# Moving the small tables and the bfloat16 constants ahead of the weight ring in SBUF

## The reference, cut to what matters

```
def sqrelu_mlp(h, w_up, w_down):          # 1024 -> 4096 -> 1024, twice
    u = jax.nn.relu(h @ w_up)
    return (u * u) @ w_down
proj = h @ w_in                           # dsa_mixer
r, k, v = jnp.einsum('cbld,cde->cble', xs[:3], w_rkv)   # rwkv7_mixer
split(h @ w_in, ...)                      # conv: 4 x 1024 columns, dilated: 8 x 1024 columns
```

## The kernel before

| tensor | start | past a whole KB |
|---|---|---|
| `raw`, `w_hi`, `w_lo` (16 KB each) | 16,512, 32,896, 49,280 | 128 |
| `X`, `const`, `const_bf` (3,328 B) | 65,664, 73,856, 86,144 | 128 |
| `gate`, `scale_row`, `pcol` | 89,472, 97,664, 101,760 | 384 |
| `mod_col` to `less_k_a` (small) | 102,688 to 103,072 | mixed |
| `per_head` | 103,104 | 704 |
| `act_f`, `act_hi0`, `act_lo0`, `act_hi1`, `act_lo1` (8 KB each), `xn` over them | from 104,128 | 704 |
| `ff_hi`, `ff_lo`, `qk` and others of the stages | from 145,088 | mostly 704 |

## Time and profile before

### The profile page before, as it was taken

One profiled execution on the slowest core, in us unless ns is written; L12 is line 12 of the kernel. 1 busy time (PEld: TensorE's weight loads), 2 busy tenths in 40 slices (PEclk: granted clock), 3 DMA queues, 4 the chain that ended last, 5 costly groups with the idle time before them and its releaser, 6 DMA issues.

```text
span 1066.7 us, 25458 instructions
## 1 busy us (share of the span) xinstructions
PE 1048.1 (98%) x10480; PEld 996.2 (93%) x10485; DVE 771.7 (72%) x1090; ACT 590.3 (55%) x900; POOL 120.4 (11%) x131
## 2 busy tenths in 40 slices
PE   9999999999999999999999999999999999999997
PEld 8966999999999899997899999999998999999985
DVE  5987666766789689768766676786676877775586
ACT  6586555555456783334555454564544667666452
POOL 0230010100000028841000000000000000000000
PEclk9999999999999999999999999999999999999999
DMA  8734687888634510002678777737653656556401
GB/s 308 251 90 137 216 286 266 271 296 280 204 122 155 163 61 5 3 11 74 217 250 287 255 252 264 276 121 228 197 192 112 212 181 199 171 195 196 143 2 59
DMA packets 83073, 192.23 MB, mean 180 GB/s; under 512 B 6000, under 2 KB 6912, under 8 KB 82992
## 3 DMA queue, kind: packets, MB, share of 16 engines
q1 hardware_dynamic: 74256, 159.93, 45.3%
q0 software_dynamic: 7584, 27.53, 7.8%
q10 hardware_dynamic: 1152, 3.59, 1.0%
HBM read 189.45 MB, written 1.05 MB: 179 GB/s over the span
## 4 chain that ended last, share of the span: by engine, by line
PE 88%; DVE 6%; issue 2%; ACT 2%; DMA 2%; POOL 0%; DVEq 0%; POOLq 0%; ACTq 0%
PE bank L2308 13%; PE bank L2310 13%; PE bank L2309 13%; PE bank L2659 5%; PE bank L2658 5%; PE bank L2660 5%; PE bank L2325 4%; PE bank L2345 4%; PE bank L2877 4%; PE bank L2275 2%; PE bank L2276 2%; PE bank L2277 2%; PE bank L2263 1%; PE bank L2265 1%; PE bank L2264 1%
## 5 line engine op out<-in xcount | busy, mean ns | idle before, releaser
L1350 DVE TENSOR_TENSOR w_lo<-raw,w_hi 128x1024 fp32r<-128x1024 f32 x295 | 357.8, 1223 | 199.2 <-ACT w_hi L737 198.7
L737 ACT ACTIVATE w_hi<-raw 128x1024 fp32r<-128x1024 f32 x295 | 310.3, 1059 | 291.4 <-PE bank L2310 150.4
L2308 PE MATMUL bank<-act_hi,w_hi 128*128 128x256 f32 x1200 | 334.0, 278 | 0.4 <-DVE w_lo L1350 0.3
L2309 PE MATMUL bank<-act_lo,w_hi 128*128 128x256 f32 x1200 | 332.9, 277 | 0.0
L2310 PE MATMUL bank<-act_hi,w_lo 128*128 128x256 f32 x1200 | 332.8, 277 | 0.0
L2308 PEld LDWEIGHTS bank<-act_hi,w_hi 128*128 128x128 f32 x1200 | 225.3, 188 | 1.7 <-DVE w_lo L1350 0.9
L2310 PEld LDWEIGHTS bank<-act_hi,w_lo 128*128 128x128 f32 x1200 | 225.3, 188 | 0.0
L2309 PEld LDWEIGHTS bank<-act_lo,w_hi 128*128 128x128 f32 x1200 | 225.0, 187 | 0.0
L2658 PE MATMUL bank<-w_hi,ff_hi 128*128 128x256 f32 x512 | 141.5, 276 | 0.0
L2659 PE MATMUL bank<-w_lo,ff_hi 128*128 128x256 f32 x512 | 141.5, 276 | 0.0
L2660 PE MATMUL bank<-w_hi,ff_lo 128*128 128x256 f32 x512 | 141.5, 276 | 0.0
(11 more groups left out here) (375 smaller groups left out, 1675.4 us busy)
## 6 DMA issues: line engine op xcount, KB each, us to landing
raw<-in_mlp_w_up_dram SPq DMA_DIRECT2D x64, 512.0 KB, 3.7
raw<-in_mlp_w_down_dram SPq DMA_DIRECT2D x64, 512.0 KB, 6.1
raw<-in_dil_w_in_dram SPq DMA_DIRECT2D x64, 512.0 KB, 4.1
mod_w<-in_w_mod_dram POOLq DMA_DIRECT2D x48, 512.0 KB, 5.9
raw<-in_conv_w_in_dram SPq DMA_DIRECT2D x32, 512.0 KB, 4.5
raw<-in_rwkv_w_rkv_dram SPq DMA_DIRECT2D x24, 512.0 KB, 4.1
raw<-in_dsa_w_in_dram SPq DMA_DIRECT2D x12, 512.0 KB, 8.1
raw<-in_dsa_w_o_dram SPq DMA_DIRECT2D x8, 512.0 KB, 4.5
```

The lines of the kernel that those rows point to most:

```text
L737: act.activation(w_hi[:, slot, :], raw[:, slot, :], ACT.Copy).then_inc(hi_ready, 1)
L1350: dve.tensor_tensor(w_lo[:, slot, :], raw[:, slot, :], w_hi[:, slot, :].bitcast(F32), ALU.subtract).then_inc(lo_ready, 1)
L2308: pe.matmul(dst, w_hi[:, slot, at], hi[:, kt, :], start=begin, stop=False, skip_group_check=True)
L2309: pe.matmul(dst, w_hi[:, slot, at], lo[:, kt, :], start=False, stop=False, skip_group_check=True)
```

## The change

The allocations of `pcol`, `mod_col`, `gain`, `c_col`, `stat`, `half_neg`, `less_k_a` and `const_bf` are moved ahead of `raw`. Nothing else is touched: no instruction, no order, no wait, no shape.

```
+        pcol = sb("pcol", [P, PARAM_COLS])
+        mod_col = sb("mod_col", [P, 2, 2 * KT])
+        ... gain, c_col, stat, half_neg, less_k_a
+        const_bf = sb("const_bf", [P, n_const_bf], BF16)
         raw = sb("raw", [P, RING, GRAN])
         ... scan_a, glora laid over w_hi and w_lo
         w_hi = sb("w_hi", [P, RING, GRAN], F32R)
         w_lo = sb("w_lo", [P, RING, GRAN], F32R)
         X = sb("X", [P, TILES, D])
         const = sb("const", [P, n_const])
-        const_bf = sb("const_bf", [P, n_const_bf], BF16)
         gate = sb("gate", [P, 2, D])
         scale_row = sb("scale_row", [P, D])
-        pcol = sb("pcol", [P, PARAM_COLS])
-        ... mod_col, gain, c_col, stat, half_neg, less_k_a
         per_head = sb("per_head", [P, SEQ])
```

More of the change, by code:

```diff
@@ L165, in program @@
         bank = [keep.enter_context(nc.psum_tensor(f"bank{b}", [P, BLOCK], F32)) for b in range(8)]
+        pcol = sb("pcol", [P, PARAM_COLS])
+        mod_col = sb("mod_col", [P, 2, 2 * KT])
+        gain = sb("gain", [P, 2, KT])
+        c_col = sb("c_col", [P, KT])
+        stat = sb("stat", [P, 26])
+        half_neg = sb("half_neg", [P, 2])
+        less_k_a = sb("less_k_a", [P, KT])
+        n_const_bf = sum(int(np.prod(v.shape[1:])) for v in parts_bf.values()) - TILES * SEQ
+        const_bf = sb("const_bf", [P, n_const_bf], BF16)
         raw = sb("raw", [P, RING, GRAN])
@@ L190, in program @@
         n_const = sum(int(np.prod(v.shape[1:])) for v in parts.values())
-        n_const_bf = sum(int(np.prod(v.shape[1:])) for v in parts_bf.values()) - TILES * SEQ
         const = sb("const", [P, n_const])
-        const_bf = sb("const_bf", [P, n_const_bf], BF16)
         gate = sb("gate", [P, 2, D])
         scale_row = sb("scale_row", [P, D])
[L196 to L202, removed]
         per_head = sb("per_head", [P, SEQ])
```

## The result

| kernel | median us | runs, us | against the kernel before, 95% interval |
|---|---|---|---|
| before | 1062.27 | 1061.30 to 1068.49 (4) | 1 |
| after | 1094.66 | 1094.29 to 1095.77 (4) | 1.0295 [1.0267, 1.0324] |

The change makes the kernel 3% slower. The forecast was no net change, 1063 us, with a range up to 1077. The measured time lies 18 us above its upper end, on the side that was given the smaller chance (0.24 for slower, 0.29 for faster).

What follows compares the result with a forecast made beforehand. The prediction took TensorE's cadence of successive products as the bound. No net change gave 1066.7 + 0 = 1066.7 us of span, carried over as a difference to 1063 us, with a range of 1048 to 1077 us.

Steps and rivals of the forecast that it cites:

- splitting, VectorE, plain float32 and the queues: Work outside split products: no cost from new addresses; at most 0.07 us on VectorE's L1426, which is not the bound.
- The two cadences at equal addresses: Split products of 256 columns: 117.7 ns in the dilated attention, 113.0 in the convolution, with the same code, tensors and addresses.
- the direct effect on the cadence: Some 6,400 split products on TensorE: moving weights to distance zero from the activations was taken to cost 0 us.
- The nearest row: The indexer's products, weights 288 B apart between slices: 117 ns, taken as the nearest evidence for distance zero.
- The bounds: All split products at the short cadence, 11.2 us less, or all at the long one, 16.3 us more.
- Modulo 512: Feature-form split products: distance alternates between 576 and 64 B with one cadence, so it could count only modulo 512 B.
- All short: Split products: alignment removes the long cadence, 11.2 us less, 1052 us; chance 0.17.
- the excess vanishes: Split products run at a plain float32 pass's pace, 46 us less, 1017 us; chance 0.12 for this or a good part.
- The MLPs stay long: Both MLPs keep the long cadence without flips, 11.2 us more, 1074 us; chance 0.16, another 0.08 for up to 1079.
- The odd pair at distance zero: MLP change from feature to token form: activations stream while ff_hi loads; this pair's address match might explain the cadence flip.
- The reshuffled cadences: Stages swap long and short cadence by less than 10.6 us, or no net change: chance 0.47, forecast 1063 us.
- The rule: TensorE reads streaming operand and next weights through independent ports, so distance cannot matter: no change; not relied on.

Runs made afterwards that it cites:

- map_forms: Separate kernel of only float32r products in an MLP step's order, at eight weight-to-activation distances: 120.0 ns at distance 0, 113.5 or 117.9 ns at 192 B.
- tables_ahead: Against the kernel before, only the small tables (1,344 B) moved ahead of the ring, const_bf left in place: 1095.34 us, ratio 1.0301.
- mod_col_ahead: Against the kernel before, only mod_col (128 B) moved ahead of the ring: 1071.93 us, ratio 1.0062.
- map_distance: Separate kernel of only float32r products, stepping the bytes by which the stationary operand lies past the streaming one: 120.0 ns at 0, 117.8 at 64 and mostly at 192.

## Why the prediction was wrong

**Right: what bounds the kernel.** It was read from the cadence of products and not from waits or busy shares, and the whole result lies in that cadence. That splitting, VectorE, plain float32 and the queues cost nothing is confirmed term by term: 1223 and 1059 ns became 1224 and 1057, L1426 and L2841 did not move. The two cadences at equal addresses are real and come back without the rest of the kernel (`map_forms`).

**The step that failed** is the one on the split products: "I therefore take **0 us** for the direct effect on the cadence." It measured +6.66 ns for each of 3,665 products and +2.21 for 2,367, and -6 for each wide one: 24.4 + 5.2 - 2.0 = +27.6 us. Four things in it were unsound.

- *The row's operands do not move.* The indexer's weights and the activations both lie behind `per_head` and keep their addresses. Its cadence is 117 ns before and after and says nothing on a change of distance.
- *The nearest row was not near.* Its products pass through distances in steps of 32 B and load 72 columns. The map shows that fewer loaded columns can take away the penalty at zero (120.0 with 128 columns, 113.4 with 64), and a mean over many distances hides the value at one. So 117 ns could not stand for distance zero.
- *The bounds were not bounds.* "The bounds are the two pure cases" took the two cadences seen today as the ends, -11.2 and +16.3 us. A row shows what holds at its own addresses. For a distance with "no steady stretch" in the trace nothing excluded a third value. The text named it as what would make the forecast wrong ("a third value") and gave it neither price nor chance.
- *Modulo 512 was the coarsest reading.* Within a granule the distance alternates between 576 and 64 B with one cadence; that allows 512 or any divisor of it. It is 256. This did not hurt the forecast of this change, as zero is zero by either, but it would have mispriced `tables_ahead`.

**The rivals.** *All short* and *the excess vanishes* had the sign wrong for the 256 columns; in the wide products alone 6 of the 16 ns did go. The observation against the latter, that wide products pay most although the load is beside only a part of them, was sound. Its price rests on 108 ns as the pace of a pass, which is half of the measured 217 and was not itself measured; the trace records each plain float32 product of the program as two (16 calls, 32 records in the earlier trace rows). No series came to it. *The MLPs stay long* had the sign right and half of the mechanism: at distance zero nothing flips any more and one cadence goes through both MLPs, 181 us each. It put that cadence at 117.8 ns; it is 120.0, in all stages. Even its farthest end, 1079, was 16 us short. The odd pair at distance zero that was to explain the flip does not by itself make one: where the token form gives way to the feature form, streaming weights meet loading weights, also at distance zero modulo 256, and the kernel before has no flip there. The reshuffled cadences that carried the chance of 0.47 exist, at the distance 64 of `mod_col_ahead`, and are worth +0.6% there.

**The rule.** By the Trainium skill (TensorE: Matmul & The Clock Gate, Part 2: What happens when you issue a matmul) streaming operand and next weights are read through two independent ports, and the load takes nothing from the stream. The maps contradict for float32r what follows from it: the same instructions take 120.0 or 113.3 ns, by their distance modulo 256 B. Whether the ports themselves or something behind them is shared, no run shows. I had seen that the trace did not agree (two cadences at equal addresses) and yet drew the rule's conclusion.

**Shown and argued.** Shown: the distance sets the cadence, with period 256 B; 0 gives 120.0 ns; amount moved, whole KB, other engines and DMA don't matter for it; the number of loaded columns does. That an operand's own place does not matter rests on the map alone, where both were moved by 64 B. Argued only: that both reads meet in some part of the memory that repeats every 256 B. What that part is, why 64 and 192 B are best, why there are two rhythms, and what sets the cadence at an entry stays open. Swapped roles are not enough for a flip, since only one direction of the change has it. They are not needed for another rhythm either, as the two series at distance 64 at the end of `map_distance` show.

## What to carry to other kernels

Where float32r products follow one another with a weight load beside each, count the cadence from start to start and look at the distance between the tensor of stationary and that of streaming operands modulo 256 B: padding of 64 B is worth 3% here. With 128 loaded columns 64 or 192 B were best. When tables are moved in such a kernel, compare this distance before and after, whatever the move is for. And where the trace has no stretch at the new operating point, the values seen at others bound nothing; give an unseen third value a price and a chance, in both directions.

## What the runs showed of the hardware

- Float32r products, 128 x 128 stationary, 256 columns streaming, clock 1.00: 120.0 ns at distance 0, 113.3 or 117.8 at 64 and 192, 113.3 to 123 elsewhere, in three kernels that do little else and in the versions of this one. With 512 columns: 227 to 228 at 0, 229 or 233 at 64 and 192.
- A stationary operand of 64 or 32 columns at distance 0: 113.4 ns; at distance 64: 119.0 with 64 columns, 113.3 with 32.
- At distances 64 and 192 two rhythms each hold for hundreds of products, 113.3 and 117.8 ns. At a change of form the cadence flips where the stationary operand's distance past the streaming one goes from 192 to 64 B (120 of 122 changes in four traces of this kernel), and not where it goes from 64 to 192 (none of 110). In one stage the cadence most likely differs between executions of the same kernel: two traces at distance 192 differ there by 6.8 us, and the times fall into two groups.
